# An expert layer on one core: when the first round's signal is given, and how the last round's sums reach the residual

## The reference

```
logits = (h @ router).astype(jnp.float32)
top_v, top_i = lax.top_k(logits, TOP_K)            # TOP_K = 2, N_EXPERTS = 8
top_w = jax.nn.softmax(top_v, axis=-1)
...
for e in range(N_EXPERTS):
    out = out + gates[..., e:e + 1] * swiglu(h, we_gate[e], we_up[e], we_down[e])
...
h = h + moe_swiglu(hn, sw_router[j], sw_we_gate[j], sw_we_up[j], sw_we_down[j])
```

## Time and profile before

| | |
|---|---|
| median of 3 runs | 1987.92 us (1987.85 to 1988.99) |
| profiled execution | 1988.2 us, of which the span of the trace is 1986.5 us |
| PE busy | 1912.8 us, 96% |
| DVE, ACT, POOL busy | 43%, 27%, 6% |
| moved by DMA | 545.32 MB, mean 275 GB/s |
| granted TensorE clock | 0.986 of full speed on the mean |

### The profile page before, as it was taken

How to read it: one execution, slowest core, us unless ns; L and a number is a source line. 1 busy time by engine, 2 the same in 40 slices (tenths; PEclk the granted TensorE clock), 3 DMA queues, 4 the chain that set the end, 5 groups by cost and what they waited for, 6 DMA issues and landing times.

```text
span 1986.5 us, 41226 instructions
## 1 busy us (share of the span) xinstructions
PE 1912.8 (96%) x17136; PEld 1243.0 (63%) x17136; DVE 861.9 (43%) x1564; ACT 544.2 (27%) x959; POOL 121.8 (6%) x139
## 2 busy tenths in 40 slices
PE   8999999999999999999995899999999999999996
PEld 7786889758888888888854244443535353444434
DVE  6577786787776986666554020201101020202011
ACT  2331356554444575545552000000000000000000
POOL 0000000000000000000201201001010202020100
PEclk9999999999999999999997899999999999999999
DMA  9788754346553416555227799999999999999993
GB/s 310 162 317 300 265 183 153 106 149 209 172 193 107 147 44 214 189 190 149 96 85 254 275 416 399 416 408 414 412 411 416 405 418 401 418 406 417 406 416 132
DMA packets 184301, 545.32 MB, mean 275 GB/s; under 512 B 32028, under 2 KB 87221, under 8 KB 159285
## 3 DMA queue, kind: packets, MB, share of 16 engines
q1 hardware_dynamic: 170877, 525.32, 69.5%
q0 software_dynamic: 8048, 13.03, 2.6%
q10 hardware_dynamic: 5208, 4.49, 1.3%
HBM read 534.00 MB, written 9.84 MB: 274 GB/s over the span
## 4 chain that ended last, share of the span: by engine, by line
PE 91%; DVE 4%; DMA 2%; ACT 1%; issue 1%; POOL 1%; SPq 0%; POOLq 0%; DVEq 0%; ACTq 0%
PE bank L1665 21%; PE sum L1682 15%; PE sum L1665 8%; PE bank L1275 7%; PE sum L1257 7%; PE bank L759 5%; PE bank L1277 4%; PE sum L823 2%; PE bank L924 2%; PE bank L777 1%; DMA hrows<-nrm 1%; PE sum L1347 1%; PE sum L803 1%; PE sum L804 1%; PE sum L805 1%
## 5 line engine op out<-in xcount | busy, mean ns | idle before, releaser
L1665 PE MATMUL bank<-ring,hg 128*32 128x512 f32 x2688 | 293.8, 596 | 26.4 <-DVE xtr L3274 26.4
L1665 PEld LDWEIGHTS bank<-ring,hg 128*32 128x32 f32 x2688 | 91.1, 111 | 220.9 <-issue 220.0
L1275 PE MATMUL bank<-hT_hl,w_hi 128*128 128x512 f32 x608 | 216.5, 399 | 2.0 <-DVE hT_hl L2465 1.3
L2488 DVE TENSOR_TENSOR w_lo<-ring,w_hi 128x1024 fp32r<-128x1024 f32 x130 | 156.0, 1223 | 77.5 <-ACT w_hi L2042 76.5
L1665 PE MATMUL sum<-x_odd,hg 128*32 128x384 f32 x2048 | 189.3, 486 | 0.0
L2042 ACT ACTIVATE w_hi<-ring 128x1024 fp32r<-128x1024 f32 x130 | 136.8, 1060 | 125.5 <-PE sum L1257 66.3
L1277 PE MATMUL bank<-hT_hl,w_lo 128*128 128x256 f32 x608 | 170.7, 281 | 0.0
L3287 DVE TENSOR_TENSOR gated<-gated,bank 128x512 f32<-128x512 f32 (+1 forms) x32 | 20.9, 655 | 340.1 <-PE bank L1665 259.9
L2302 ACT ACTIVATE ey<-sum,gate_of 128x256 f32<-128x256 f32 x24 | 11.4, 474 | 501.6 <-PE sum L1682 497.2
L1682 PE MATMUL sum<-ring,actT 128*32 128x256 f32 x2688 | 146.5, 379 | 0.0
L3278 DVE COPY gate_of<-row_table 128x3 f32<-128x3 f32 x8 | 1.4, 170 | 332.6 <-DMA xrows<-ey,targeti 332.6
(11 more groups left out here) (643 smaller groups left out, 2995.1 us busy)
## 6 DMA issues: line engine op xcount, KB each, us to landing
ring<-in_sw_we_gate SPq DMA_DIRECT2D x56, 1024.0 KB, 9.4
ring<-in_sw_we_up SPq DMA_DIRECT2D x56, 1024.0 KB, 10.3
ring<-in_sw_we_down SPq DMA_DIRECT2D x56, 1024.0 KB, 10.6
x_odd<-in_sw_we_gate SPq DMA_DIRECT2D x64, 768.0 KB, 8.1
x_odd<-in_sw_we_up SPq DMA_DIRECT2D x64, 768.0 KB, 10.7
x_odd<-in_sw_we_down SPq DMA_DIRECT2D x64, 768.0 KB, 9.7
ring<-in_w_in SPq DMA_DIRECT2D x36, 1024.0 KB, 9.0
ring<-in_w_ff SPq DMA_DIRECT2D x32, 1024.0 KB, 5.5
```

Of the source, the lines that this page charges most:

```text
L1275: mm(o[:, :].rearrange("p (a n) -> p a n", a=2), hi[:, k, cols], hT_hl[:, :, kk, :], start=(kk == 0), stop=False)
L1665: last = mm(wide_banks[half][x][32 * q:32 * q + 32, 0:n], hg[:, k, 32 * x:32 * x + 32], w[:, n * q:n * (q + 1)], start=(k == 0), stop=(k = ...
L2488: v.tensor_tensor(w_lo[:, hp % SPLITS, :], ring[:, W.place(key), lo:lo + PIECE // 2], w_hi[:, hp % SPLITS, :].bitcast(F32), ALU.subtract). ...
```

## The change

Two edits.

1. The signal for PE's first expert product is given by an instruction some 60 operations earlier on DVE (the sum of the two gates' exponents, L3207), and the small copy that gave it (L3274) goes.
2. The last round's sums no longer go to DRAM by indirect DMA. After the rounds SP loads `xrows`, which holds all the rounds but the last, back into `xres`. DVE writes for each token its number 4 x token + q and compares it with each slot's target: `gated[0]` then has, for each of the three tiles, 128 slots (32q + s) by 256 tokens, with a one where slot and token belong together. PE multiplies these with `ey`: for each tile, half of the tokens (t) and quarter (q) a product over 32 partitions into `ps[q]`, 24 in all. DVE adds each of the four banks to `xres`, and SP stores the output from there in four pieces of 256 columns.

```
-                sp.wait_ge(c.sem("last_added"), 16 * TILES)
-                sp.dma_start(out.rearrange("a s d -> (a s) d"), xrows[0:S, :]).then_inc(c.sem("out_stored"), 16)
-                sp.wait_ge(c.sem("out_stored"), 16)
-                return
...
+                c.loop = n_rounds - 1
+                sp.wait_ge(*c.at("rows_added", TILES - 1))
+                c.loop = None
+                sp.dma_start(xres[:, :, :], xrows[0:S, :].rearrange("(t p) d -> p t d", p=P)).then_inc(c.sem("x_back"), 16)
+            for q in range(4):
+                sp.wait_ge(*c.at("x_ready", q))
+                sp.dma_start(out.rearrange("a (t p) d -> p (a t) d", p=P)[:, :, 256 * q:256 * q + 256],
+                             xres[:, :, 256 * q:256 * q + 256]).then_inc(c.sem("out_stored"), 16)
+            sp.wait_ge(c.sem("out_stored"), 64)
...
         @block.tensor
...
+            pe.wait_ge(*c.at("tokens_marked"))
+            for x in range(TILES):
+                pe.wait_ge(*c.at("ey_last", x))
+                for t in range(NT):
+                    for q in range(4):
+                        last = mm(ps[q][:, 256 * t:256 * t + 256], gated[0][32 * q:32 * q + 32, x, t * P:(t + 1) * P],
+                                  ey[32 * q:32 * q + 32, x, :], start=(x == 0 and t == 0), stop=(x == TILES - 1 and t == NT - 1))
+                        if x == TILES - 1 and t == NT - 1:
+                            last.then_inc(c.sig(f"last_placed{q}").sem, 1)
...
         @block.vector
...
-            do(v.tensor_reduce(xtr[:, 0:NT, 1], rt[:, 4, :, :], AX, ALU.add))
+            do(v.tensor_reduce(xtr[:, 0:NT, 1], rt[:, 4, :, :], AX, ALU.add), c.sig("rows_turned", "first"))
...
-            do(v.tensor_copy(xtr[:, 6, 3:4], ones[:, 0:1]), c.sig("rows_turned", "first"))
...
+            c.loop = n_rounds - 1
+            do(v.tensor_copy(target[:, :], targeti[:, :]))
+            for t in range(NT):
+                token = gated[1][:, 0, t * P:(t + 1) * P]
+                do(v.tensor_scalar(token, C("iota"), 4.0, C("quads")[:, TILES:TILES + 1], ALU.mult, ALU.add))
+                if t:
+                    do(v.tensor_scalar(token, token, float(4 * P * t), None, ALU.add))
+            for x in range(TILES):
+                do(v.tensor_scalar(gated[0][:, x, 0:S], gated[1][:, 0, 0:S], target[:, x:x + 1], None, ALU.is_equal),
+                   c.sig("tokens_marked") if x == TILES - 1 else None)
+            dve.wait_ge(c.sem("x_back"), 16)
+            for q in range(4):
+                dve.wait_ge(*c.at(f"last_placed{q}"))
+                do(v.tensor_tensor(xres[:, :, 256 * q:256 * q + 256], xres[:, :, 256 * q:256 * q + 256],
+                                   ps[q][:, :].rearrange("p (t n) -> p t n", t=NT), ALU.add), c.sig("x_ready", q))
...
         @block.gpsimd
...
-            for x in range(TILES):
-                pool.wait_ge(*c.at("ey_last", x))
-                g.indirect_dma_start(xquads, bass.IndirectOffsetOnAxis(ap=targeti[:, x:x + 1], axis=0), ey[:, x, :], None, compute_op=ALU.add)\
-                    .then_inc(c.sem("last_added"), 16)
```

## The result

The changed kernel took 1957.77 us (median of 4 runs, 1956.69 to 1959.84), the kernel before 1988.19 us beside it (1987.85 to 1988.99). The ratio is 0.9848, 95% interval 0.9831 to 0.9865: 30.4 us less, where 30 were forecast.

The account below looks back on a forecast made before the run. PE sets the pace, with DMA also full in the rounds; time is won only where PE stands still. From 1988.2 us, less 25.6, 0.7 and 3.7, against the median: 1958 us, range 1954.5 to 1966.

Parts of the forecast that it names:

- PE's start, behind ACT's copy: Start of the rounds: PE's first expert product follows ACT's `hg` copy by 0.27 us, 25.6 us earlier.
- clock and rounds: Start of the rounds: less time lost at half clock, 0.7 us saved, between nothing and 2.45.
- weights: Weight stream in the last rounds: spare of 8.5 us falls by 6.8 to 9.3; no loss, 3.5 us far bound.
- the end: From PE's last expert product to the span's end: 11.2 us instead of 14.9, 3.7 us less.
- rival 3: Start of the rounds: something other than the signal holds PE until about 1100; 1984 us, chance 0.05.
- POOL's chain: Entries, tables and zero adds beside the weight stream: 25 us before; even doubled it stays hidden, some 7 us left.
- rival 4: First round: POOL's work in the stream holds DVE, which holds PE at `down_sums`; 1992 us and more, chance 0.03.
- Rival 1: Last rounds: the weight stream starves PE, costing 1 to 3.5 us, 1959 to 1961.5 us; chance 0.2.
- the store: At the end: SP's last 256 KB lands in 3.6 us, with 0.5 less as the low bound.
- rival 2: Last products: row groups don't overlap, 7.5 us more, chance 0.1; or only two at a time, 3 us more, 0.1.
- `x_back`: 1 MB load ahead of DVE's first add at the end: hidden, with a thin cover of 3 to 5 us.
- the 0.48: Chance given to the forecast itself, whole kernel, with its own range of 1955 to 1961 us.

Follow-up runs that it names:

- `group_by_group`: The changed kernel with the two inner loops of the last products swapped, so neighbouring products share a row group; one execution, span 1954.3 us, products 3.08 us.
- `signal_only`: The kernel before with only the signal for PE's first expert product moved earlier; ratio to the kernel before 0.9873, 25 us less.
- `warm_gather`: The changed kernel with three idle PE products in the wait ahead of the first tokens' gather; ratio to the kernel before 0.9849.

## Why the prediction was right

The sizes are those of the profiles, by the prediction's own terms.

| term | predicted | measured |
|---|---|---|
| PE's start, behind ACT's copy | −25.6 | −25.7 (0.10 us of wake instead of 0.27; before 1101.50 − 1075.67) |
| clock and rounds | −0.7, within 0 to −2.45 | +0.4 (870.51 against 870.09 us); −0.9 in `group_by_group` |
| weights | 0, spare between +1.7 and −0.8 | 0, spare 0.9 |
| the end | −3.7 (11.2 us) | −5.5 (9.4 us) |
| upstream, not part of the change | – | +2.4 in this execution |
| sum | −30.0 | −28.4, the two spans (1986.5, 1958.1); by the medians −30.4 |

**Edit 1** went as forecast. The wait that it removed had nothing behind it, so rival 3 is out, and `signal_only` gives its size alone: 25 us. POOL's chain took 1130.3 − 1089.6 = 40.7 us from its first entry instead of 25, in the weight stream, less than the doubled 50 that the prediction allowed, and DVE waited 8.3 us for PE behind it: rival 4 is out.

**The clock** is the term with the wrong sign, by 1.1 us in this execution and outside the bounds that the prediction gave it. The mechanism is the prediction's own: half of the time at 0.50 is lost. But the rise did not come sooner with PE's early start. It came 5.7 us behind it instead of 4.9, and half of the difference is the +0.4. Over the twelve profiles it lies between 3.1 and 5.7 us behind PE's start, so the 0.7 was a guess inside that scatter. The Trainium skill (TensorE: Matmul & The Clock Gate, Part 1), which the prediction set beside it, has activity release the throttle. In both kernels the clock rose while PE worked without a gap; but the gather ahead of it, nearly 8 us of busy PE at a granted clock that had just fallen to 0.50, did not bring the rise forward.

**The weight stream** is the step that mattered most and could have gone the other way. The prediction said that PE moves forward more than the stream and that the spare falls from 8.5 us by 6.8 to 9.3. It fell from 8.0 by 7.1, to 0.9. That this is the mechanism, and not an incidental row, is shown by the added loads: the same 512 KB a round cost 3.2 us of the rounds before and 10.6 after. Rival 1 was wrong by less than one microsecond: no loss came of it, but by a thin margin, and an execution with an early rise of the clock already had 0.5 us of wait (`warm_gather`). SP's issues took longer too, 1.33 us for the last `x_even` up piece against 0.33 before, and the eight last `x_odd` pieces 19.67 us against 15.29. So a landing counted from the issue hides a part of the lateness. Why the issues take longer no view shows; a queue that is full would do it.

**The end** was mis-sized by 1.8 us in the right direction. The term that was off is the store: 2.3 us for 256 KB against the 3.6 that loads of that size had taken, each of which was the last of seven loads issued for one weight piece. Whether it is the direction or those loads' neighbours that makes the difference was not tested. The products span 2.87 us (2.9 + 0.16 predicted), PE was awake 0.15 us sooner, the adds took 2.85 (2.9), and the remaining 0.1 us is in the wakes. Row groups of 32 overlap nearly four at a time (3.6), more than the two groups of 64 in the earlier trace rows could show; rival 2 is out in both its forms. The Trainium skill's figure of 3.07 for four row groups (TensorE: Matmul & The Clock Gate, Part 3, for products of 512 columns) would have been 3.4 us; the run, with 256, shows 10.4 / 2.87 = 3.6.

`x_back` was no matter: it was in at 1926.93 + 16.2 = 1943.1, 9 us ahead of DVE's first add, where the prediction had a cover of 3 to 5. It had counted 3 to 6 us from the landing of the last weight pieces, at up to 1941; the load was issued at 1926.93, before these were in.

That the total came out within 0.3 us owes something to chance: the end won 1.8 us more than forecast and the clock 1.1 less, which nearly cancel, and the executions lie up to 3.2 us apart (1956.69 to 1959.84), the profiled one 1.6 above the forecast for it. A slip in the prediction's chances is without weight: with rivals 1 to 4 and the 0.48 they add up to 0.96, which leaves 0.04 and not 0.06.

## What to carry to other kernels

A wait can hold one engine while the other full resource, here the weight stream, uses the time to get ahead. Taking the wait away is then worth its length only as long as the lead lasts. Compute the lead at the end of the stream, where it is smallest, from one landing time and one release time, and test it with a load that nobody reads. And look at what releases a long wait: here it was a signal given by an instruction that had nothing to do with what was waited for.

## What the runs showed of the hardware that was not expected

- A gather by products whose weights are read with a stride of eight elements took 7.94 us with the granted clock at 0.50 for nearly all of it, and 7.77 us with the clock at full for over half of it.
- In a stream of 411 GB/s the time from issue to landing grew by 2.1 us a round of 109 us in the kernel before (8.1 to 22.5 us) and by 2.4 in the changed one. Behind the last issues the DMA share then stands near one half (0.52 over 15 us in the kernel before). Indirect adds are not the cause, the indirect gathers have a part in it.
- SP's issue of an `x_even` piece took 0.33 us in the kernel before and 1.33 in the last round of the changed one, and four stores of 256 KB one after the other took 2.00 us, some 0.5 each.
- The granted clock has short spells at half (1.2 GHz) ahead of the rounds, with PE busy most of the time, and not the same ones in each execution: over 985 to 1010 us its mean was 0.93 in the kernel before and in the changed one, 1.00 in `group_by_group` and `warm_gather`, which is up to 0.07 x 25 = 1.8 us of PE's time (an estimate). Three of these are as much as the end's whole gain.
